# Query units spread past the peer boundary, and TensorE's slots 0.6 batches later with six diagonals

## The reference

```python
q = (xb @ w_query).reshape(PEER_BLOCK, PEER_HEADS, 2, PEER_HALF)
sc = jnp.einsum('thcd,hcnd->thcn', q, sub_keys).astype(jnp.float32)
top_s, top_i = lax.top_k(sc, PEER_TOPK)
...
best_s, best_j = lax.top_k(cand.reshape(PEER_BLOCK, PEER_HEADS, -1), PEER_TOPK)
idx = jnp.take_along_axis(cand_idx.reshape(PEER_BLOCK, PEER_HEADS, -1), best_j, axis=-1)
gate = jax.nn.softmax(best_s, axis=-1)
u = jnp.take(expert_u, idx, axis=0)
h = jax.nn.gelu(jnp.einsum('td,thkd->thk', xb, u).astype(jnp.float32), approximate=False)
wgt = (gate * h).astype(xb.dtype)
return jnp.einsum('thk,thkd->td', wgt, jnp.take(expert_v, idx, axis=0))
```

## Time and profile before

| | us |
|---|---|
| median of 3 runs (3160.76 to 3165.59) | 3164.18 |
| the profiled execution | 3158.0 |
| its span, first to last instruction | 3156.2 |
| TensorE busy | 2636.7 (84%) |
| VectorE busy | 2311.6 (73%) |
| DMA: 1259.44 MB, mean | 399 GB/s |

### The profile page before, as it was taken

One profiled execution on the slowest core, in us unless ns is written; L12 is line 12 of the kernel. 1 busy time (PEld: TensorE's weight loads), 2 busy tenths in 40 slices (PEclk: granted clock), 3 DMA queues, 4 the chain that ended last, 5 costly groups with the idle time before them and its releaser, 6 DMA issues.

```text
span 3156.2 us, 30754 instructions
## 1 busy us (share of the span) xinstructions
PE 2636.7 (84%) x8024; PEld 1422.0 (45%) x8024; DVE 2311.6 (73%) x4961; ACT 947.5 (30%) x3082; POOL 1246.4 (39%) x1060
## 2 busy tenths in 40 slices
PE   8889988899988888988999887988877676666666
PEld 7766666565544445544444454533332222222222
DVE  2487768898766677889787667788978886666666
ACT  2123413334332232333443223232322232222222
POOL 0122343334444443433334333434544444454452
PEclk9989999999999999999999999999999998888888
DMA  9999999999999999999999999999999999999997
GB/s 291 250 404 362 352 418 398 386 419 418 420 419 417 420 388 410 420 420 396 397 345 407 419 420 417 411 411 419 413 421 421 414 409 421 421 417 415 422 422 311
DMA packets 204708, 1259.44 MB, mean 399 GB/s; under 512 B 31228, under 2 KB 34892, under 8 KB 68976
## 3 DMA queue, kind: packets, MB, share of 16 engines
q0 software_dynamic: 152064, 1107.36, 85.5%
q1 hardware_dynamic: 49856, 144.24, 12.7%
q10 hardware_dynamic: 2616, 5.88, 0.5%
HBM read 1251.72 MB, written 5.79 MB: 398 GB/s over the span
## 4 chain that ended last, share of the span: by engine, by line
DMA 43%; PE 31%; DVE 16%; issue 4%; ACT 3%; DVEq 1%; POOL 1%; SPq 1%; ACTq 0%; POOLq 0%
DMA ring<-in_uv,idx 38%; PE acc L1040 15%; PE wide L1021 10%; DVE ring L1308 7%; DMA wring<-in_w_q 3%; DVE acc_v L1319 2%; DMA wring<-in_w_a 1%; PE wide L1207 1%; PE wide L1234 1%; DVEq L1292 1%; PE wide L1135 1%; POOL ring L793 1%; PE wide L1117 1%; ACT diag L838 1%; PE wide L1277 1%
## 5 line engine op out<-in xcount | busy, mean ns | idle before, releaser
L793 POOL DMA_INDIRECT ring<-in_uv,idx x1056 | 1246.2, 1180 | 1880.8 <-PE acc L1040 1383.1
L1040 PE MATMUL acc<-ring,diag 128*128 128x512 f32 (+1 forms) x3308 | 1632.1, 638 | 406.6 <-ACT diag L838 381.8
L1308 DVE CUSTOM_DVE_ANT_0 ring<-ring,xb 128x1024 f32<-128x1024 f32 x1056 | 1275.5, 1224 | 558.6 <-DMA ring<-in_uv,idx 515.2
L1040 PEld LDWEIGHTS acc<-ring,diag 128*128 128x128 f32 (+1 forms) x3308 | 638.8, 200 | 1265.3 <-issue 1240.5
L824 ACT ACTIVATE hgelu<-hdot 128x2 f32<-128x2 f32 x528 | 107.2, 203 | 1793.9 <-DVE hdot L1308 1793.6
L1021 PE MATMUL wide<-xm,wring 128*128 128x256 f32 (+5 forms) x2352 | 613.7, 412 | 29.3 <-DMA wring<-in_w_q 24.2
L1021 PEld LDWEIGHTS wide<-xm,wring 128*128 128x128 f32 x2352 | 432.2, 199 | 221.4 <-issue 107.2
L1319 DVE SCALAR_TENSOR_TENSOR acc_v<-ring,hw,acc_v 128x1024 f32<-128x1024 f32 x229 | 294.1, 1284 | 28.8 <-ACT hw L827 7.0
L838 ACT ACTIVATE diag<-ident,hw 128x128 f32<-128x128 f32 x801 | 292.1, 396 | 73.1 <-PE acc L1040 30.9
L827 ACT ACTIVATE hw<-hgelu,gate 128x1 f32<-128x1 f32 x1056 | 253.7, 287 | 37.6 <-issue 1.4
L1234 PE MATMUL wide<-wring,big 128*128 128x256 f32 (+1 forms) x536 | 125.0, 387 | 3.1 <-DMA wring<-in_w_a 3.1
(11 more groups left out here) (196 smaller groups left out, 1310.5 us busy)
## 6 DMA issues: line engine op xcount, KB each, us to landing
wring<-in_w_a SPq DMA_DIRECT2D x141, 512.0 KB, 7.9
wring<-in_w_q SPq DMA_DIRECT2D x64, 576.0 KB, 8.2
ring<-in_uv,idx POOLq DMA_INDIRECT x1056, 16.4
ring<-in_w_a SPq DMA_DIRECT2D x27, 512.0 KB, 8.4
xb<-in_x_rows SPq DMA_DIRECT2D x8, 512.0 KB, 13.7
out_y_prompt<-xb ACTq DMA_DIRECT2D x8, 512.0 KB, 7.8
att<-in_ln_g SPq DMA_DIRECT2D x4, 512.0 KB, 12.4
att<-in_ln_b SPq DMA_DIRECT2D x4, 512.0 KB, 15.7
```

The lines of the kernel that those rows point to most:

```text
L793: pool.indirect_dma_start(ring[:, s % RING, :], None, uv, bass.IndirectOffsetOnAxis(ap=idx[:, n % LISTS, j:j + 1], axis=0))\
L1040: k = mm(acc[0:width, c * 512:(c + 1) * 512], diag[:, r % DIAGS, 0:width], ring[:, s % RING, D + c * 512:D + (c + 1) * 512], start=(s == f ...
L1308: V.tensor_tensor_reduce(u, u, x, 1.0, 0.0, ALU.mult, ALU.add, hdot[:, k, j:j + 1])\
```

## The change

`Clock` spreads a group's items in two stretches in place of one. The first stretch runs up to query unit `SPLIT[g]` (2 for group 1, 4 for groups 2 and 3) and ends `LEAD[g]` batches ahead of the group's first peer (12, 14, 14); it begins `TAIL[g-1]` batches behind the start of the group before's first peer. The other query units follow up to `TAIL[g]` batches (8, 8, 12) behind the start of the first peer. Group 0's formula gives the same places as before. Peer 1's retrieval gets five parts in place of four (heads 0, 1, 2 to 3, 4 to 5, 6 to 7), and a group's first peers have their gates' softmax in three or four parts in place of two. `DIAGS` goes from 4 to 6, and TensorE's slots of batch m stand at m+1.6. `plan_sums`, unchanged itself, sees the new places. Empty lines of the diff are left out.

```diff
--- before.py
+++ after.py
@@ -53,7 +53,7 @@
 BATCH = 2
 BATCH0 = [s // BATCH for s in SLOT0]
 RING = 10
-DIAGS = 4
+DIAGS = 6
 SMALL = 4
 ROWS = 5
 
@@ -145,7 +145,7 @@
 
 
 
-BY = [[(0, 2)] if b < 0 else [(0, 1), (1, 2), (2, 4), (4, 6), (6, 8)] if n == 0 else [(0, 2), (2, 4), (4, 6), (6, 8)]
+BY = [[(0, 2)] if b < 0 else [(0, 1), (1, 2), (2, 4), (4, 6), (6, 8)] if n < 2 else [(0, 2), (2, 4), (4, 6), (6, 8)]
       for n, b in enumerate(PEERS)]
 
 STEPS = [[(u, 0, n) for u in range(16)] for n in SIZES]
@@ -161,7 +161,15 @@
 NORM0 = -28.0
 
 
+SPLIT = (0, 2, 4, 4)
+LEAD = (0, 12, 14, 14)
+TAIL = (6.2, 8, 8, 12)
 class Clock:
 
 
 
@@ -194,17 +202,19 @@
             items.append((pos, cost[pos], 0))
         items.append(("norm", 0, (2.7 + 1.2 * blocks) * self.q))
         items += [(("query", k), (wide + 32 * SIZES[g]) if g else 0, 0) for k in range(len(STEPS[g]))]
-        us = sum(x[1] for x in items)
-        gaps = sum(x[2] for x in items)
-        begin = BATCH0[peer_of(FIRST[g - 1])] if g else 0
-        if g == 1:
-            begin += 6.2
-        end = BATCH0[peer_of(FIRST[g])] - (3 if g == 1 else 0) if g else 0
-        scale = (end - begin - gaps) / us if g else 0.7 * 0.01334
+        split = [x[0] for x in items].index(("query", SPLIT[g]))
         self.place = {}
-        for key, cost, gap in items:
-            self.place[key] = begin
-            begin += cost * scale + gap
+        if g:
+            first = BATCH0[peer_of(FIRST[g])]
+            bounds = [BATCH0[peer_of(FIRST[g - 1])] + TAIL[g - 1], first - LEAD[g], first + TAIL[g]]
+            stretches = [(items[:split], *bounds[0:2]), (items[split:], *bounds[1:3])]
+        else:
+            stretches = [(items, 0, 0.7 * 0.01334 * sum(x[1] for x in items) + sum(x[2] for x in items))]
+        for part, begin, end in stretches:
+            scale = (end - begin - sum(x[2] for x in part)) / sum(x[1] for x in part)
+            for key, cost, gap in part:
+                self.place[key] = begin
+                begin += cost * scale + gap
         if g == 1:
             self.place[POS_K] = NORM0 + 0.4
         if g == 0:
@@ -294,15 +304,17 @@
 def plan_gates():
 
     out = []
-    for n in range(len(PEERS)):
-        for k, (a, z) in enumerate(BY[n]):
-            at, step = RETRIEVAL[n][k]
-            if n and PEERS[n] != FIRST[group_of(PEERS[n])] and z < BY[n][-1][1]:
-                continue
-            if n and n != SAMPLES and k % 2 == 0:
-                continue
-            if n and n != SAMPLES:
-                a = z - 4 if PEERS[n] == FIRST[group_of(PEERS[n])] else 0
+    for n, b in enumerate(PEERS):
+        if b < 0:
+            spans = BY[n]
+        elif n == 0:
+            spans = BY[n]
+        elif b == FIRST[group_of(b)]:
+            spans = BY[n][:-2] + [(4, 8)]
+        else:
+            spans = [(0, 8)]
+        for a, z in spans:
+            at, step = RETRIEVAL[n][[x[1] for x in BY[n]].index(z)]
             out.append((n, a, z, at + 13 * step + 0.1))
     return out
 
@@ -1026,7 +1038,7 @@
                     width = SAMP if n == SAMPLES else P
                     first, last = SLOT0[n], SLOT0[n + 1] - 1
                     for m in range(BATCH0[n], BATCH0[n + 1]):
-                        yield m + 0.99
+                        yield m + 1.6
                         for s in range(BATCH * m, BATCH * m + BATCH):
                             if on_dve(s):
                                 continue
```

## The result

The changed kernel took 3180.05 us, median of seven runs (3173.38 to 3186.54), beside 3163.96 for the kernel before in seven. The ratio is 1.0053, with a 95% interval from 1.0041 to 1.0064: 0.5% slower, where 0.4% faster was forecast. The time lies 2 us above the end of the range. The profiled execution took 3178.83. Lines of the changed kernel's code stand 12 further on: L1052 is TensorE's slots, L1289 and L1287 are the scores (L1287 those of the samples' group), L1257 and L1260 the turns (the transposes of a normed row that the query units then read), L1139 the transposes of the softmax, L999 ScalarE's evacuation of a query, which is its copy out of TensorE's result.

The account below looks back on a forecast made before the run. DMA at about 420 GB/s over 1259 MB sets the floor, with time lost where TensorE returns ring tiles late. -11.0 -5.3 +0 +3 +2 +0 = -11.3 us on the 3164.2 median gives 3153; range 3125 to 3178.

Parts of the forecast that it names:

- Part 1: Batches 48 to 64: query units leave the end of peer 0, stretch becomes DMA-bound; -11.0 us (bounds 0, -15).
- batch 64 at about 590: Sign of being right: batch 64 would start at about 590 us in place of 601.
- Part 2: Work ahead of queries spread thinner: -5.3 us in 274:383 (bounds 0, -8), 0 for group 3 (-5, +6).
- Part 3: Moved work's arrival: +3 us in batches 64 to 112 and +2 in 336 to 348, each 0 to +6.
- Part 4: TensorE's slots at m+1.6: less waiting for diagonals traded against waiting elsewhere; 0 us (bounds -6, +37).
- B: Rival, slower: TensorE idles at softmax transposes, slots queued behind, both attention stretches; 25 us against 11, 3178; chance 0.20.
- 8 us of queue cover: Where DMA is the bound, gather latency can fall from 16.5 to 8.3 us, hiding the 3 us later release.
- Part 5: Small items: six diagonals, more softmax parts, no gather waiting for indices, SP's queue; all at 0.
- A: Rival, displaced: moved work starves the ring in 656:877, costing what was won; about 3164, no change; chance 0.25.
- C: Rival, more won: VectorE's score waits vanish, attention stretches recover a third to half of 48 us; about 3133; chance 0.15.
- the rate behind batch 336: Sign of being wrong: a rate under 400 GB/s in batches 336 to 348.
- the idle before the transposes: Sign of being wrong: TensorE's idle there well above 16.6 us; about 12 us extra would decide for B.

Follow-up runs that it names:

- run 1: Changed kernel with TensorE's slots back at m+0.99 and four diagonals, query units' new places kept; 3147.78 us, ratio 0.9949 to the kernel before.
- run 5: Changed kernel, slots still at m+1.6, with scores, turns, softmax transposes and products with v of groups 1 to 3 moved 0.61 batches later; 3149.55 us.
- run 6: New places, slots at m+0.99, four diagonals, with scores, turns, softmax transposes and products with v 0.61 batches earlier; 3210.29 us, ratio 1.0138.
- run 3: Changed kernel with four diagonals in place of six; 3180.04 us, ratio 1.0058 to the kernel before.
- run 4: New places for group 1 alone, slots at m+0.99, four diagonals; group 2 evenly from batch 72 to 192, group 3 as before; 3143.29 us.

## Why the prediction was wrong

The prediction priced parts 1 to 3 as loss: the length of a stretch times the rate missing from 421 GB/s. A stretch also becomes shorter when loads move out of it, and that time comes back where they land. So the two have to be kept apart here.

**Part 1, the query units ahead of batch 64: right, in mechanism and size.** -11.0 was forecast. In run 1 batches 48 to 64 lose 0.4 us in place of 11.0, at 419 GB/s, with TensorE busy 86.7 us where about 93 had been forecast: DMA-bound, as was said. The stretch itself became 19 us shorter, 113 to 94: besides the 10.6 us of loss, by length times rate it moves 39.4 MB in place of 42.9, which is 8 us. 94 us is what the prediction's own count of 95 us of DMA need gave. Its sign "batch 64 at about 590" subtracted only the 11 us from 601 and left out these loads and part 2; it was 575 in run 1, 578 in the changed kernel.

**Part 2, the thinner front: right for group 1, and for group 3 in sum.** Batches 16 to 32 lost 22.5 us before and 16.5 in run 1, 6 us for 5.3 forecast:

```profile
270.00:372.00 102.00, 96.93 (x350) 62.52 (x349) 82.69 (x176) 44.77 (x125) 33.21 (x29) 0.99 0.92 353
```

For group 3 the zero held, but not as it was argued: the 25.6 us lost in batches 212 to 249 fell to 9.2 in the changed kernel, and 15.4 were lost in 248 to 264, which had lost nothing.

**Part 3, the landing: right at group 1, too small at group 3.** Batches 64 to 112 took 276 us before and 285 in run 1, but 6 of these 9 us are bytes that came in; by loss it is +2.7 where +3 stood. Batches 336 to 352 lost 5.8 us more, where 2 stood, near the bound of 6:

```profile
635.00:860.00 225.00, 215.56 (x684) 124.06 (x683) 190.81 (x510) 74.95 (x246) 92.11 (x80) 0.99 1.01 419
```

The parts without the later slots were summed to -11.3. Run 1 measured -17.0 by the medians and -11.5 from profile to profile. The close agreement is in part luck: these stretches alone give about -8, and the rest lies where zero was forecast.

**Part 4, the later slots: this is the step that failed.** It stood at 0, between -6 and +37, and it measured +16.6 on the old places and +32 on the new. The bounds held it, but the range that was stated did not use them: it ended at B's 3178, while the sum with +37 in it leads to 3190. The value was chosen by setting two kinds of waiting off against each other because their rows were of like size. They are not of one kind. When TensorE waits for a diagonal, what is held up is that very slot, which is not ready anyhow; nearly nothing of value stands behind it. That is argued from the order; the runs show that the time does not follow these waits. When it waits at a score, what stands behind it are slots that are ready, and ring tiles that GpSimd could fill. Runs 5 and 6 show from both sides that these waits cost. The forecast also counted only the softmax, as the place where TensorE comes too early, and gave for it. That was the smallest of the three: it rose by 6.8 us, the scores' wait by 32.4, the turns' by 21.0. All three could have been read off the order: a score waits for an evacuation that ScalarE lists 0.1 batches ahead of it, behind the dot products of that same batch, so with the slots 0.6 later up to one batch more of ready slots is queued behind it. And the claim that 8 us of queue cover hides a 3 us later release took the delay to be 3 us; a single stop was 9.31.

**Part 5 held.** GpSimd waited for indices once, at the start (137.0 us, 136.8 before), and four diagonals take the time of six (run 3).

**The rivals.** B, slower by a wait at TensorE with slots queued behind, is what happened, with 0.20 of the chance. Its place was wrong, scores and turns and not the softmax in the attention stretches, and that its 3178 is 2 us off is luck: it is 25 us at the softmax against 11 won, where 32 at all the waits stand against 17, and the softmax rose by 6.8. A, displacement, is a smaller part of it: batches 64 to 72 and 336 to 352 in run 1. C did not come: VectorE's waits for scores did fall, from 22.1 us to 8.9 in the changed kernel, but the 20 us that C hung on them are not there. Rival A drew on the rule by which TensorE's headroom is judged by weight-load time (and by the share of peak arithmetic), not by matmul busy time (the Trainium skill, "Perfetto Trace Analysis", Identifying the Most-Contended Engine). Run 1 answers what was drawn from it: at 65% of weight-load time TensorE did hold 488:601 back, and with 17.6 us less of its work the rate went from 380 to 419 GB/s. Of the prediction's own signs of being wrong the rate behind batch 336 came, 371 GB/s where 400 was set; the idle before the transposes rose by 6.8 us, short of the 12 that were to decide for B. A slip without weight: 656:877 lost 1.0 us at 419 GB/s, not 0.3.

**What stays open.** How the 17 us of run 1 split between the units' tail and the thinner front was not tried apart, nor what the planner's new choice of who sums which slot does by itself; batches 212 to 249 in run 4 suggest some 8 us. How much of run 5's missing gain its stop at the first query unit explains was not tried. Why the later slots cost more on the new places than on the old is only argued: more of the scores then lie where retrieval and the closing of a peer make VectorE late, as at 591 to 603.

## What to carry to other kernels

In an in-order engine that serves a ring, a wait costs by what is queued behind it: let it stop at the step that the ring itself needs, and put steps that need a fresh result of another engine late enough that the result is there. Moving one kind of work later in such a list is the same as moving all others earlier, so each of these has to be looked up with what it waits for and how far that stands behind in the other engine's list. Two waits of the same length in a profile may be set off against each other only if the same work stands behind both.
